# Transposing the attention probabilities two heads ahead in a float32 diffusion backbone step

## The reference, cut to what matters

```python
def one_block(args):
    bi, qblk = args
    ...
    l_ctx = jnp.einsum('bqkgd,bskd->bkgqs', qf, kc) * scale
    l_band = jnp.einsum('bqkgd,bskd->bkgqs', qf, kb) * scale
    l_band = jnp.where(mask[None, None, None], l_band, -jnp.inf)
    p = softmax_with_sink(jnp.concatenate([l_ctx, l_band], axis=-1), s_sink)
    return (jnp.einsum('bkgqs,bskd->bqkgd', p[..., :Lc], vc)
            + jnp.einsum('bkgqs,bskd->bqkgd', p[..., Lc:], vb))
```

## Time and profile before

| quantity | value |
|---|---|
| timed executions | 2183.78, 2191.92, 2192.34 us |
| their median | 2191.92 us |
| the profiled execution's own time | 2190.16 us |
| its span, first to last instruction | 2188.3 us |
| outside the span | 1.9 us |
| mean granted TensorE clock over the span | 0.975 |

### The profile page before, as it was taken

The page is one execution under the profiler, slowest core; times in us unless marked ns, Lnnn a source line. Parts: engine busy times, 40 slices in busy tenths (PEclk is TensorE's granted clock), DMA queues, the critical chain, the costliest instruction groups (busy, mean ns, idle before and its releaser), DMA issues.

```text
span 2188.3 us, 30546 instructions
## 1 busy us (share of the span) xinstructions
PE 2063.0 (94%) x13110; PEld 1947.3 (89%) x13110; DVE 1163.6 (53%) x1699; ACT 761.7 (35%) x1118; POOL 161.5 (7%) x180
## 2 busy tenths in 40 slices
PE   4989998899999999999998999799999999999997
PEld 2468888799998999999998888689999999999996
DVE  5523456775746677777644545772335533234435
ACT  2253344532226331133225344452224533123323
POOL 0020000000015000000023000010003300000011
PEclk8999999999999999999999999899999999999999
DMA  5423112144421334533321110221221121222121
GB/s 227 160 90 109 39 37 87 49 140 140 154 97 59 135 142 144 206 141 135 137 83 68 61 37 20 106 68 58 87 78 66 70 78 54 92 78 78 60 67 48
DMA packets 33871, 207.07 MB, mean 95 GB/s; under 512 B 4054, under 2 KB 4615, under 8 KB 15048
## 3 DMA queue, kind: packets, MB, share of 16 engines
q1 hardware_dynamic: 29320, 185.02, 23.8%
q10 hardware_dynamic: 3120, 11.99, 1.4%
q0 software_dynamic: 1296, 8.11, 1.0%
HBM read 196.98 MB, written 8.13 MB: 94 GB/s over the span
## 4 chain that ended last, share of the span: by engine, by line
PE 86%; DVE 6%; ACT 5%; issue 2%; DMA 1%; POOL 0%; SPq 0%; ACTq 0%; DVEq 0%; POOLq 0%
PE gemm_psum L574 50%; PE gemm_psum L604 14%; PE gemm_psum L624 3%; PE gemm_psum L587 3%; PE aux_psum L689 3%; PE gemm_psum L642 3%; PE aux_psum L674 2%; PE aux_psum L741 2%; PE gemm_psum L514 2%; PE gemm_psum L729 1%; PE gemm_psum L467 1%; ACT h_src_rows L1080 1%; PE aux_psum L698 1%; PE aux_psum L498 1%; ACT w_hi L1028 1%
## 5 line engine op out<-in xcount | busy, mean ns | idle before, releaser
L574 PE MATMUL gemm_psum<-h_hi,w_hi 128*128 128x322 f32 x2176 | 505.9, 314 | 9.4 <-DVE gates L1763 3.9
L574 PE MATMUL gemm_psum<-h_hi,w_lo 128*128 128x322 f32 x2176 | 502.4, 312 | 0.0
L574 PE MATMUL gemm_psum<-h_lo,w_hi 128*128 128x322 f32 x2176 | 501.3, 312 | 0.0
L1456 DVE TENSOR_TENSOR w_lo<-w_raw,w_hi 128x2048 fp32r<-128x2048 f32 (+2 forms) x144 | 287.7, 1998 | 306.7 <-ACT w_hi L1028 305.0
L574 PEld LDWEIGHTS gemm_psum<-h_hi,w_hi 128*128 128x128 f32 x2176 | 369.6, 190 | 15.1 <-issue 10.6
L574 PEld LDWEIGHTS gemm_psum<-h_lo,w_hi 128*128 128x128 f32 x2176 | 369.6, 190 | 0.0
L574 PEld LDWEIGHTS gemm_psum<-h_hi,w_lo 128*128 128x128 f32 x2176 | 369.1, 190 | 0.0
L1028 ACT ACTIVATE w_hi<-w_raw 128x2048 fp32r<-128x2048 f32 (+2 forms) x144 | 239.5, 1663 | 170.4 <-PE gemm_psum L604 65.6
L1444 DVE CUSTOM_DVE_ANT_0 aux_psum<-w_raw,cond_by_row 128x1024 f32<-128x1024 f32 x160 | 191.0, 1256 | 4.2 <-DMA w_raw<-in_ada_t 4.0
L1573 DVE SCALAR_TENSOR_TENSOR x<-gemm_psum,mod,x 128x128 f32<-128x128 f32 (+2 forms) x144 | 55.3, 434 | 164.8 <-PE gemm_psum L604 131.4
L604 PE MATMUL gemm_psum<-act_hi,w_lo 128*128 128x322 f32 x616 | 141.9, 311 | 0.0
(11 more groups left out here) (298 smaller groups left out, 3249.5 us busy)
## 6 DMA issues: line engine op xcount, KB each, us to landing
w_raw<-in_w_up SPq DMA_DIRECT2D x44, 1024.0 KB, 4.8
w_raw<-in_ada_t SPq DMA_DIRECT2D x40, 1024.0 KB, 4.8
w_raw<-in_w_down SPq DMA_DIRECT2D x32, 704.0 KB, 4.1
w_raw<-in_w_gate SPq DMA_DIRECT2D x16, 1024.0 KB, 4.8
w_raw<-in_w_z SPq DMA_DIRECT2D x12, 1024.0 KB, 4.7
w_raw<-in_ada SPq DMA_DIRECT2D x8, 1024.0 KB, 4.9
w_raw<-in_w_proj SPq DMA_DIRECT2D x16, 512.0 KB, 3.3
w_raw<-in_w_out SPq DMA_DIRECT2D x8, 1024.0 KB, 4.7
```

Of the source, the lines that this page charges most:

```text
L574: last = mm(gp[:, 2 * (t % 2) + hf, 0:HALF], w[:, off + P * kk:off + P * (kk + 1)], moving(kk, lo)[:, hf * HALF:(hf + 1) * HALF], start=kk ...
L1456: TT(wlo[s][:, 0:n], raw[STEP[(lane.layer, "g", g)] % 2][:, 0:n], f32(whi[s][:, 0:n]), ALU.subtract).then_inc(sem["w_split"], raised("w_sp ...
```

## The change

A third buffer `p_t_third` is laid into SBUF behind the attention's other tiles, in space that the Hyena stage uses later, and PSUM bank 3 joins banks 0 and 1 for the transposes. Buffers and banks go by `n % 3`. TensorE's order becomes

```diff
@@ memory
             ca = sb("z_acc", [P, 2, ROW], F32, s2)
+            pt_third = sb("p_t_third", [P, 4 * P], F32, s2)
@@
+    p_t = lambda n: pt_third if n % 3 == 2 else pt[:, n % 3, :]
+    pt_bank = lambda n: ax[:, (0, 1, 3)[n % 3], :]
@@ TensorE, tpv(b)
-                    last = mm(ax[:, 2, HD * n:HD * (n + 1)], pt[:, n % 2, P * kb:P * (kb + 1)],
+                    last = mm(ax[:, 2, HD * n:HD * (n + 1)], p_t(n)[:, P * kb:P * (kb + 1)],
...
             for n in range(NH):
                 pe.wait_ge(sem["exp_out"], due("exp_out", NH * b + n + 1))
+                for kb in range(nk):
+                    last = tr(pt_bank(n)[:, P * kb:P * (kb + 1)], sc[:, n, P * kb:P * (kb + 1)], ident[:, :])
+                last.then_inc(sem["pt_mm"], raised("pt_mm"))
                 if n >= 2:
-                    pe.wait_ge(sem["pt_dve" if n % 2 else "pt_act"], due("pt_dve" if n % 2 else "pt_act", (NH // 2) * b + n // 2))
-                for kb in range(nk):
-                    last = tr(ax[:, n % 2, P * kb:P * (kb + 1)], sc[:, n, P * kb:P * (kb + 1)], ident[:, :])
-                last.then_inc(sem["pt_mm"], raised("pt_mm"))
-                if n:
-                    pv(n - 1)
+                    pv(n - 2)
+            pv(NH - 2)
             pv(NH - 1)
@@ ScalarE, tpv(b), even heads
-                if NH * b + n >= 2:
-                    act.wait_ge(sem["pv_mm"], due("pv_mm", NH * b + n - 1))
-                run(pt[:, 0, 0:nk], ax[:, 0, 0:nk], ACT.Copy).then_inc(sem["pt_act"], raised("pt_act"))
+                if NH * b + n >= 3:
+                    act.wait_ge(sem["pv_mm"], due("pv_mm", NH * b + n - 2))
+                run(p_t(n)[:, 0:nk], pt_bank(n)[:, 0:nk], ACT.Copy).then_inc(sem["pt_act"], raised("pt_act"))
@@ VectorE, tpv(b), odd heads
-                if NH * b + n >= 2:
-                    dve.wait_ge(sem["pv_mm"], due("pv_mm", NH * b + n - 1))
-                V.tensor_copy(pt[:, 1, 0:nk], ax[:, 1, 0:nk]).then_inc(sem["pt_dve"], raised("pt_dve"))
+                if NH * b + n >= 3:
+                    dve.wait_ge(sem["pv_mm"], due("pv_mm", NH * b + n - 2))
+                V.tensor_copy(p_t(n)[:, 0:nk], pt_bank(n)[:, 0:nk]).then_inc(sem["pt_dve"], raised("pt_dve"))
```

## The result

| | before | after |
|---|---|---|
| median, us | 2190.11 (2183.78 to 2196.41, 10 runs) | 2177.89 (2174.32 to 2185.12, 10 runs) |
| ratio after / before | | 0.9948, 95% interval 0.9935 to 0.9962 |
| profiled execution, us (its span) | 2190.16 (2188.3) | 2177.99 (2176.2) |
| mean granted clock of the span | 0.975 | 0.981 |

The medians differ by **12.2 us, 0.56%**; the interval of the ratio puts the saving between 8.3 and 14.2 us. The forecast was 2175.0 in a range of 2170 to 2185; its sum of 16.0 is 3.8 too large.

The account below looks back on a forecast made before the run. TensorE's own work was taken to bound the kernel, so only closed gaps or a higher clock pay. Blocks 1 to 4 5.1 + block 0 2.0 + clock 8.9 = 16.0 us off 2190.2 gave 2174.2, stated as 2175, range 2170 to 2185.

Parts of the forecast that it names:

- the last head: End of blocks 1 to 4: last copy gets two `pv` to hide behind; saves 0.30 or 0.20 us a block.
- The third transpose in the idle stretch: Start of blocks 1 to 4: T2 runs ahead of `pv0` while TensorE waits; saves 0.34 or 0.44 us a block.
- two take 2 x 0.61: End of a block with 3 key blocks: two `pv` need 1.22 us where 1.62 passes, so 0.40 is lost.
- Block 0: First block of each layer: deeper order shortens `pv0` to logits, 3.35 to 2.4 us; about 1.0 a layer, 2 in all.
- The granted clock: Behind block 0 in both layers: the falls to half clock go away, saving 8.9 us.
- I take 8.9, since the nearest rows are block 1's: Behind block 0: full 8.9 us taken, as block 1 kept its clock after 1.30 us idle and dense work.
- the sign by which the prediction had said it would know itself wrong in this term: Behind block 0 in the profile after: granted clock still 0.50 would refute the sum's largest term, 8.9 us.
- The rival of one fall left: Behind block 0: the clock still falls in one layer only; about 2179 us, chance 0.22.
- The range: Whole kernel: 2170 to 2185 us, covering no fall, one fall or both falls left behind block 0.
- The rival of a slower kernel: Stalls of blocks 1 to 4: new clock falls at 3.8 to 5.2 us each, up to 2205 us; chance 0.04.
- The rival of no gain: Whole attention: copies were hidden already and T2 only changes places; 2189 us, chance 0.06.
- the stall that stays: Start of each block: `pv0` waits while ScalarE runs `z_acc` before copy 0; waits 13.0 us, forecast about 9.5.

Follow-up runs that it names:

- The two kernels with filler: Needless TensorE products put in the idle stretch ahead of each block's first `pv`: on the kernel before 2187.86 us, on the kernel after 2181.40 us.

## Why the prediction was nearly right

The bound was right: TensorE, closed gaps and the clock, and nothing of another engine or a transfer came in their way. The waits and the block lengths came out near where they were put; the sum was 3.8 us too high, nearly all of it in two terms, the last head and the clock.

- **The third transpose in the idle stretch**: forecast 0.34 and 0.44 a block; in the whole order 0.33 and 0.43 (0.53 and 0.54 less the end's 0.20 and 0.11).
- **The last head**: forecast 0.30 and 0.20 a block, measured 0.20 and 0.11, so 0.53 and 0.54 in place of 0.64 for the two together, and 4.3 us for 5.1 in all. The mis-sized step is what stays of the loss. The forecast left 0.10 for the waits ahead of the logits; 0.15 stays there (0.76 for 0.61). And "two take 2 x 0.61" prices a `pv` by a row in which transposes stood between, while `pv` behind `pv` takes 0.67, and with 4 key blocks 0.89 for 0.84. The timeline of the kernel after shows both with 4 key blocks, 0.89 from `pv6` to `pv7` and 0.99 to the logits, end of block 2 in layer 0:

```profile
299.03 0.39 PE L692 MATMUL aux_psum<-par,p_t 128*128 128x64 f32 x2
...
299.92 0.39 PE L692 MATMUL aux_psum<-par,p_t 128*128 128x64 f32 x2
...
300.91 0.50 PE L677 MATMUL aux_psum<-kcT,q 64*128 64x128 f32 x4
```

- **Block 0**: 3.46 to 2.52 at the full clock in layer 1, 0.94 a layer for 1.0, built up from handovers and steps; 1.9 for 2.0. The two kernels with filler give 0.92 in layer 0 (3.66 and 2.74).
- **The granted clock**: forecast 8.9, about 5.6 by difference in the medians. The mis-sized step is "I take 8.9, since the nearest rows are block 1's". The price of the falls was right: in the profiled pair 13.1 - 6.2 = 6.9 goes to the clock, and the fall that is left costs some 1.5 more (0.27 and 1.19), 8.4 for 8.9. Their number was wrong. The prediction assumed that the profiled execution's two falls are what each execution before has, and that none is left after. Neither holds: the same old block 0 kept its clock in one layer of the kernel with only blocks 1 to 4 changed, and the kernel after lost it in layer 0 of its own profile, the sign by which the prediction had said it would know itself wrong in this term. The rival of one fall left, put at about 2179 with the remark that the falls may come and go between executions, described the profiled execution better than the forecast did; the median of 2177.9 lies between the two. That 2175 came within 2.9 of it owes something to luck: the term that carried more than half of the sum was a choice between 0 and 8.9.
- **The range**: the spread of the runs goes with the falls of the clock (before 12.6 us, after 10.8; 3.5 and 3.7 with filler), so the upper edge of 2185 was needed, for the execution at 2185.1. A median below 2181 had a chance of 0.68, and came.
- **The rival of a slower kernel** had a real mechanism: falls behind the stalls of blocks 1 to 4 exist, at 4.7 us. Two were seen, in one profiled execution with the old order and two banks, where idle time of 1.30 stands ahead; the profile after shows none in these blocks. In which share of executions they come isn't known.
- **The rival of no gain** is out: the kernel before with filler and the one after with filler differ by 6.5 us with the clock level in the attention of both profiles.
- **What the prediction passed over**: it named ScalarE's `z_acc` as the stall that stays, and left it there. It was the largest wait of the attention, 13.0 us, and the trace showed VectorE idle beside it (4.63 us).

## What to carry to other kernels

When a matmul waits at the head of a block for a copy that stands behind another job in its engine's queue, look first for an engine that is idle there; here the deeper pipeline left that wait in place and paid at the two ends of a block and where the pieces are shorter than a copy. Don't price an order by a duration from a row with other neighbours, and price the step to what follows the last piece too: find a row with the same neighbours, or bound it. And before a clock fall in one profile is booked as a gain, ask how many executions have it: set the mean granted clock of each run beside its time, and where the two go together compare kernels with the idle time filled or gone.

## What the runs showed of the hardware

The granted clock is no fixed property of the kernel. In the runs of the kernel before, those at 2183.1 to 2185.2 us had a mean granted clock of 0.979 to 0.981, those near 2191 mostly 0.974 to 0.976, and those at 2200.1 to 2202.7 had 0.970 or 0.971; in the kernel after, 2174.3 to 2176.5 went with 0.984, and 2183.8 and 2185.1 with 0.977. A fall to 0.50, 1.2 in place of 2.4 GHz, began 1.6 to 2.5 us behind the end of an idle time of 1.3 to 1.5 us in the kernels before, after and with only block 0 changed (there the idle time ended at 259.55, and the fall began at 261.20); in the kernel before, the same idle time of 1.30 ended at 263.70 in the same block, and no fall came. The falls that began in the attention of these three kernels lasted 3.4 to 17.2 us, also where TensorE was busy throughout (13.60 of 13.60 us in the kernel with only block 0 changed), where the prediction had expected them only with gaps behind. An idle time as long as that isn't needed either: in the kernel with VectorE's first copies and the old order, the waits in block 0 of layer 1 were 0.27 and 0.41, and the clock fell behind it. Stretch of that kernel:

```profile
1244.30:1251.10 6.80, 6.80 (x33) 5.63 (x33) 3.96 (x12) 0.60 (x1) 0.00 (x0) 0.50 0.00 0
```

Four kernels showed no fall in the attention of their profiles: the two with filler, and the two with the new order and VectorE's first copies. Which of the remaining idle times brings a fall, and why one execution has it and the next doesn't, was not settled. What it can be worth shows in the filler: needless work that cost 1.7 us a layer left the median of the kernel before no slower (0.9993, 0.9980 to 1.0007), and no fall was left in the attention of its profile.
